# The up product of two MLPs with its operands swapped: weight blocks stationary, both parts of the input moving together

## The reference, cut to what matters

```python
def sq_relu_mlp(x, w_up, w_down):
    h = jax.nn.relu(x @ w_up)
    return (h * h) @ w_down

    # in second_block, for layers 0 and 1
    h = h + rms_norm(sq_relu_mlp(rms_norm(h, mpre), w_up, w_down), mpost)
```

## Time and profile before

| | |
|---|---|
| device time, median of 3 runs | 1142.04 us (1142.02 to 1142.12) |
| device time of the profiled execution | 1141.86 us |
| its span (first to last instruction) | 1140.0 us |
| PE busy | 1130.2 us (99%) |
| PEld busy | 935.3 us (82%) |
| DVE, ACT, POOL busy | 656.9, 622.5, 180.9 us |
| DMA | 204.57 MB, mean 179 GB/s |

### The profile page before, as it was taken

How to read it: one execution, slowest core, us unless ns; L and a number is a source line. 1 busy time by engine, 2 the same in 40 slices (tenths; PEclk the granted TensorE clock), 3 DMA queues, 4 the chain that set the end, 5 groups by cost and what they waited for, 6 DMA issues and landing times.

```text
span 1140.0 us, 14044 instructions
## 1 busy us (share of the span) xinstructions
PE 1130.2 (99%) x5299; PEld 935.3 (82%) x5299; DVE 656.9 (58%) x680; ACT 622.5 (55%) x786; POOL 180.9 (16%) x123
## 2 busy tenths in 40 slices
PE   8999999999999999999999999999999999999998
PEld 7788888888888888888778888888888888888886
DVE  5735668675655544784348565454465776744442
ACT  6655556654867643644478374443355546655331
POOL 1423500000434310000032021110015100211000
PEclk9999999999999999999999999999999999999999
DMA  9644344554554554655335456445545324655530
GB/s 354 237 154 164 131 166 156 194 185 185 185 190 179 192 190 171 231 221 194 139 120 194 150 212 223 176 180 189 198 186 206 128 110 166 221 184 182 184 114 37
DMA packets 30322, 204.57 MB, mean 179 GB/s; under 512 B 3584, under 2 KB 3744, under 8 KB 6592
## 3 DMA queue, kind: packets, MB, share of 16 engines
q1 hardware_dynamic: 28752, 198.75, 48.3%
q0 software_dynamic: 1520, 5.12, 1.4%
HBM read 202.81 MB, written 1.05 MB: 179 GB/s over the span
## 4 chain that ended last, share of the span: by engine, by line
PE 94%; POOL 1%; issue 1%; DVE 1%; ACT 1%; DMA 1%; SPq 0%; DVEq 0%; POOLq 0%; ACTq 0%
PE ps L654 84%; PE aux L726 3%; PE aux L1163 1%; PE ps L776 1%; PE aux L939 1%; PE aux L925 1%; DMA mrows<-in_mem 1%; POOL sc L498 0%; PE aux L1093 0%; PE aux L1044 0%; DVE Wl L1794 0%; ACT Wh L1267 0%; POOL sq L514 0%; DVE sc L1866 0%; ACT prob L1444 0%
## 5 line engine op out<-in xcount | busy, mean ns | idle before, releaser
L1794 DVE TENSOR_TENSOR Wl<-raw,Wh 128x2048 fp32r<-128x2048 f32 x184 | 427.6, 2330 | 326.6 <-ACT Wh L1267 326.3
L654 PE MATMUL ps<-Wh,xT 128*128 128x512 f32 x1920 | 608.2, 393 | 0.0
L1267 ACT ACTIVATE Wh<-raw 128x2048 fp32r<-128x2048 f32 x184 | 349.9, 1907 | 266.5 <-PE ps L654 265.6
L654 PEld LDWEIGHTS ps<-Wh,xT 128*128 128x128 f32 x1920 | 360.5, 188 | 75.1 <-issue 1.2
L654 PE MATMUL ps<-Wl,xT 128*128 128x512 f32 x960 | 373.7, 389 | 0.0
L654 PEld LDWEIGHTS ps<-Wl,xT 128*128 128x128 f32 x960 | 180.4, 188 | 36.4 <-issue 0.5
L654 PE MATMUL ps<-Wh,hTh 128*128 128x512 f32 x256 | 100.1, 391 | 0.0
L654 PE MATMUL ps<-Wh,hTl 128*128 128x512 f32 x256 | 99.7, 389 | 0.0
L654 PE MATMUL ps<-Wl,hTh 128*128 128x512 f32 x256 | 99.6, 389 | 0.0
L654 PEld LDWEIGHTS ps<-Wh,hTl 128*128 128x128 f32 x256 | 48.0, 188 | 10.0
L654 PEld LDWEIGHTS ps<-Wl,hTh 128*128 128x128 f32 x256 | 48.1, 188 | 9.9
(11 more groups left out here) (347 smaller groups left out, 1219.2 us busy)
## 6 DMA issues: line engine op xcount, KB each, us to landing
raw<-in_wstream SPq DMA_DIRECT2D x185, 1024.0 KB, 4.7
grow<-in_post_gains POOLq DMA_DIRECT2D x4, 512.0 KB, 5.5
grow<-in_b_gate POOLq DMA_DIRECT2D x6, 256.0 KB, 3.5
mrows<-in_mem SPq DMA_DIRECT2D x2, 512.0 KB, 5.1
raw<-in_wstream SPq DMA_DIRECT2D x2, 512.0 KB, 6.4
x<-in_x SPq DMA_DIRECT2D x1, 1024.0 KB, 13.3
out<-x SPq DMA_DIRECT2D x4, 256.0 KB, 2.0
rdm<-in_ret_decays POOLq DMA_DIRECT2D x1, 768.0 KB, 6.9
```

The lines of the kernel that those rows point to most:

```text
L654: mm = nc.tensor.matmul(ps[2 * pair + t][:, :], a[:, kt, t * P:(t + 1) * P], w[:, slot, j, :], start=(first and j == 0 and q == 0), stop=( ...
L1267: nc.scalar.activation(Wh[:, slot, 0:nk, :], raw[:, slot, 0:nk, :], ACT.Copy).then_inc(hi_ready, 1)
L1794: nc.vector.tensor_tensor(Wl[:, slot, 0:nk, :], raw[:, slot, 0:nk, :], Wh[:, slot, 0:nk, :].bitcast(F32), ALU.subtract).then_inc(lo_ready, 1)
```

## The change

Up units 0 and 1 stay as they were. For units 2 to 7 of both MLPs:

- **PE.** The 128 x 128 blocks of `Wh` and `Wl` are stationary. For each of four groups of 128 output columns (c = 0 to 3) and each of eight feature steps there is one matmul of `Wh` with both parts of x side by side (512 wide), and one of `Wl` with the high part (256 wide, into the first half of the bank). Column c fills one bank, `column_bank`, whose halves have to be added. The result has output columns on partitions, so it is already transposed: `turned` remains for units 0 and 1 alone. A granule is given back in the last column.
- **`xT`** is laid out with the two parts of each feature step side by side.
- **DVE** adds the halves of each bank into `hrow` (`add_parts`), and subtracts the rounded square from the square for the low part (`rows_low`), both from SBUF, 1024 wide, for the unit before.
- **ACT** applies relu in place in SBUF (`relu`), and later squares the scaled rows in place and rounds them to `hTh` (`rows_high`).
- **POOL** multiplies the rows with `rstd` of each token (`scaled`) instead of squaring. As tokens lie along the row now, `rstd` is needed in every partition: DVE writes two diagonal matrices (`diagonal`), PE multiplies them with ones (`spread_rstd`), DVE copies the result into `spread`, once an MLP.
- Unit 2 and unit 3 are written out, the loop has two turns.

```diff
-        xT = at("xT", [P, 2, DK, TOK], 104, F32R)
-        xTh, xTl = xT[:, 0, :, :], xT[:, 1, :, :]
+        xT = at("xT", [P, DK, 2, TOK], 104, F32R)
+        xTh, xTl = xT[:, :, 0, :], xT[:, :, 1, :]
...
+        def column_bank(m, c):
+            return ps[(2 * U[f"up{m}_0"] + c) % 4]
...
+                def scaled(n, count):
+                    pool.wait_ge(drained["act"], count * 2 + (DRAIN[f"up{m}_0"][1] + 2))
+                    h = hrow[:, n, :, :].rearrange("p b (c t) -> p (b c) t", t=TOK)
+                    nc.gpsimd.tensor_tensor(h, h, spread.unsqueeze(1).broadcast_to([P, 4, TOK]), ALU.mult)\
+                        .then_inc(sem("h_scaled"), 1)
...
                 def up(n, i):
                     name = f"up{m}_{n}"
-                    for q in range(2):
-                        g = G[name] + q
-                        granule(g % RING, i * 4 + (g + 1), xTh, xTl, range(4 * q, 4 * q + 4), U[name] % 2, q == 0, q == 1,
-                                read_out)
+                    for c in range(4):
+                        if isinstance(i, int) and n == 0:
+                            pe.wait_ge(drained["act"], reads(f"up{m}_{c // 2}", c % 2))
+                        else:
+                            pe.wait_ge(sem("column_read"), i * 8 + (4 * n + c + 24 * m - 11))
+                        o = column_bank(m, c)
+                        for kt in range(DK):
+                            g = G[name] + kt // 4
+                            if c == 0 and kt % 4 == 0:
+                                pe.wait_ge(lo_ready, i * 4 + (g + 1))
+                            w = slice(c * P, (c + 1) * P)
+                            nc.tensor.matmul(o[:, :], Wh[:, g % RING, kt % 4, w], xT[:, kt, :, :], start=(kt == 0), stop=False,
+                                             skip_group_check=True)
+                            mm = nc.tensor.matmul(o[:, 0:TOK], Wl[:, g % RING, kt % 4, w], xTh[:, kt, :], start=False,
+                                                  stop=(kt == DK - 1), skip_group_check=True)
+                            if c == 3 and kt % 4 == 3:
+                                mm.then_inc(gran_used, 1)
+                            elif kt == DK - 1:
+                                mm.then_inc(half_done if c == 1 else sem("column_done"), 1)
...
+                def spread_rstd():
+                    pe.wait_ge(sem("rstd_diag"), 2 * m + 2)
+                    o = open_aux(f"rs{m}")
+                    for t in range(2):
+                        mm = nc.tensor.matmul(o[:, t * P:(t + 1) * P], K("ones"), spread[:, t * P:(t + 1) * P], start=True, stop=True)
+                    done(mm, f"rs{m}")

                 turned(0)
-                with pe.Fori(1, 4) as i:
+                spread_rstd()
+                up(0, 1)
+                turned(1)
+                up(1, 1)
+                with pe.Fori(2, 4) as i:
                     up(0, i)
-                    turned(-1, i)
                     up(1, i)
-                    turned(0, i)
...
+                def rows_high(n, i):
+                    act.wait_ge(sem("h_scaled"), i * 2 + (n + 6 * m - 1))
+                    h = hrow[:, n % 2, :, :].rearrange("p b c -> p (b c)")
+                    nc.scalar.activation(h, h, ACT.Square).then_inc(sem(f"h{m}_rows"), 1)
+                    act.wait_ge(sem(f"h{m}_rows"), i * 2 + (n + 1))
+                    dst = hTh[:, :, :].rearrange("p (n k) t -> p n (k t)", k=4)
+                    nc.scalar.activation(dst[:, i * 2 + n, :], h, ACT.Copy).then_inc(sem(f"h{m}T_hi"), 1)
...
+                def columns(n, i, between):
+                    name = f"up{m}_{n}"
+                    relu(n, i, 0)
+                    between()
+                    split(G[name] + RING, i)
+                    relu(n, i, 1)
+                    split(GEND[name] - 1 + RING, i)
...
+                columns(0, 1, lambda: h_high(1))
+                columns(1, 1, lambda: rows_high(0, 1))
+                with act.Fori(2, 4) as i:
+                    columns(0, i, lambda: rows_high(-1, i))
+                    columns(1, i, lambda: rows_high(0, i))
                 split(G[f"down{m}_0"] + RING)
-                h_high(7)
+                rows_high(1, 3)
...
+                    o = column_bank(m, c)
+                    nc.vector.tensor_reduce(hrow[:, n, c // 2, (c % 2) * TOK:(c % 2 + 1) * TOK],
+                                            o[:, :].rearrange("p (q t) -> p t q", q=2), AX.X, ALU.add).then_inc(sem("column_read"), 1)

+                def columns(n, i, between):
+                    for c in range(3):
+                        add_parts(n, i, c)
+                    between()
+                    add_parts(n, i, 3)
+                    up(n, i)
```

More of the change, by code:

```diff
@@ L177, in plan_aux @@
     use("x3T", [0, 1, 2, 3])
-    for n in range(8):
-        use(f"h0T{n}", [2 * n % 4, 2 * n % 4 + 1])
+    use("h0T0", [0, 1])
+    use("rs0", [2])
+    use("h0T1", [2, 3])
     use("x4T", [0, 1, 2, 3])
@@ L191, in plan_aux @@
     use("x5T", [0, 1, 2, 3])
-    for n in range(8):
-        use(f"h1T{n}", [2 * n % 4, 2 * n % 4 + 1])
+    use("h1T0", [0, 1])
+    use("rs1", [2])
+    use("h1T1", [2, 3])
     return plan
@@ L369, in build @@
         hrow = at("hrow", [P, 2, 2, C], R + 64)
+        spread0 = CONST["chunk_upto"][0]
+        spread = cst[:, spread0:spread0 + TOK]
         junk = at("junk", [P, D], R + 72)
@@ L604, in squares, with one @@
             def squares(m):
-                def one(n, count):
-                    pool.wait_ge(drained["act"], 2 * count + (DRAIN[f"up{m}_0"][1] + 2))
-                    h = hrow[:, n % 2, :, :]
+                def one(n):
+                    pool.wait_ge(drained["act"], 2 * n + (DRAIN[f"up{m}_0"][1] + 2))
+                    h = hrow[:, n, :, :]
                     nc.gpsimd.tensor_tensor(h, h, h, ALU.mult).then_inc(sem(f"h{m}_rows"), 1)
-                one(0, 0)
-                one(1, 1)
-                with pool.Fori(1, 4) as i:
+                def scaled(n, count):
[3 more added lines that the diff above has]
+                        .then_inc(sem("h_scaled"), 1)
+                one(0)
+                one(1)
+                wait_read(pool, f"rs{m}")
+                scaled(0, 2)
+                scaled(1, 3)
+                with pool.Fori(2, 4) as i:
                     for n in range(2):
-                        one(n, i * 2 + n)
+                        scaled(n, i * 2 + n)
             after_mix("p2", "x3", (1, reads("reto1", 1)))
@@ L679, in kts_of, with product @@
                 return range(k0, k0 + KTS[g])
-            def product(name, operand, before=None, leave=0):
+            def product(name, operand, before=None, leave=0, bank_free=None):
                 th, tl = operand
@@ new lines, in turned @@
+                def turned(n):
+                    pe.wait_ge(sem(f"h{m}_rows"), n + 1)
+                    for b in range(2):
+                        turn(f"h{m}T{n}", b, [(kk * TOK + t * P, hrow[:, n, t, (2 * b + kk) * P:(2 * b + kk + 1) * P])
+                                              for kk in range(2) for t in range(2)])
+                def spread_rstd():
[4 more added lines that the diff above has]
+                    done(mm, f"rs{m}")
@@ L1175, in go_on @@
                     def go_on():
-                        if q == 1:
-                            turned(7)
-                        wait_operand(f"h{m}T{q}", range(2))
-                    return go_on
-                product(f"down{m}_0", (hTh, hTl), before={q: before(q) for q in range(8)})
-                product(f"down{m}_1", (hTh, hTl), leave=RING)
+                        if q < 2:
+                            wait_operand(f"h{m}T{q}", range(2))
+                        else:
+                            pe.wait_ge(sem("h_low"), 6 * m + q - 1)
@@ L1183, in mlp @@
+                    return go_on
+                product(f"down{m}_0", (hTh, hTl), before={q: before(q) for q in range(8)}, bank_free=column_free(0))
+                product(f"down{m}_1", (hTh, hTl), leave=RING, bank_free=column_free(1))
                 tile_by_tile(steps_of([f"down{m}_1"], (hTh, hTl)),
@@ L1680, in up, with relu @@
                         nc.scalar.activation(hrow[:, n % 2, t, :], bank(name, t), ACT.Relu,
                                              scale=S(f"{xname}_rstd", t, t + 1)).then_inc(drained["act"], 1)
-                    split(GEND[name] - 1 + RING, i)
-                def h_high(n, i=None):
+                    split(GEND[name] - 1 + RING)
+                def relu(n, i, b):
+                    act.wait_ge(sem("column_read"), i * 8 + (4 * n + 2 * b + 2 + 24 * m - 8))
+                    h = hrow[:, n, b, :]
+                    nc.scalar.activation(h, h, ACT.Relu).then_inc(drained["act"], 1)
@@ L1685, in h_high @@
+                def h_high(n):
                     dst = hTh[:, :, :].rearrange("p (n b k) t -> p n b k t", b=2, k=2)
                     for b in range(2):
```

(18 more changed lines are left out.)

59 lines of the change are left out of this document (27 added, 32 removed).

## The result

| | median | ratio to before |
|---|---|---|
| before | 1142.09 us | |
| changed kernel | 1144.55 us | 1.0021 [1.0013, 1.0028] |

What follows compares the result with a forecast made beforehand. PE's stream was taken to bound the kernel, then a DVE-ACT-POOL round of 11.95 us against PE's 11.20. Saving 1.65 us in each MLP took 1141.86 to 1138.6, forecast as 1138.8 us; range 1134.8 to 1147.5.

Steps and rivals of the forecast that it cites:

- a closed round of DVE, ACT and POOL: Per changed unit, in-order queues tie these engines into a round of 11.95 us, where PE needs 11.20.
- PE's own sum: PE alone, per MLP: dearer matmul pairs (0.350 us each) and `spread_rstd` against six transpose groups dropped: -3.0 us, both -6.1.
- rival 3: On PE, loads aren't hidden behind 256-wide matmuls: 0.415 us a pair, 13.3 a unit, +18.9, total 1161 us; chance 0.06.
- rival 1: DVE-ACT-POOL round of 10.6 us keeps up with PE, no waits: -6.1, or -7.2 at 0.347 a pair; chance 0.16.
- Adds of halves, roundings, relu, square, copy, low part: DVE and ACT operations: `add_parts` 0.683 us, roundings 1.92 or 1.81, relu 0.63, square and copy 1.06 each, `rows_low` 1.22.
- rival 2: DVE's `add_parts` is dear: gain nothing at 0.83 us, total +10.3 at 1.22; 1144 to 1152 us; chance 0.22.
- The port: POOL and DVE exclude each other when DVE has two SBUF inputs; after the wait POOL takes 1.75 us, DVE 2.14.
- Hand-overs of 0.03: Between ACT and DVE in the round, one engine's end to the next one's start takes 0.03 us.
- Rival 4: Nothing measurable: hand-overs of 0.1, or square and copy 0.3 us longer, make the round about 12.3: -1.5 to +1; chance 0.21.
- Sum: Whole program: 1.65 us saved in each MLP, -3.3 from 1141.86 gives 1138.6; median 0.18 above, so 1138.8 us.
- The delay at the start: First changed units: ACT's `h_high(1)` waits for `turned(1)`, ending about 695.7; add 3 of the second unit ends 709.5.

Runs made afterwards that it cites:

- the fourth experiment: Changed kernel with one more wait, so POOL starts `scaled` only after DVE's second subtraction of weights of the unit; all work kept: 1134.59 us, 0.9935 of the kernel before.
- The first experiment: Changed kernel with POOL multiplying the rows by themselves, one SBUF tensor instead of two, scaling by rstd left out: 1139.62 us, 0.9978 of the kernel before.

## Why the prediction was wrong

The direction was wrong; the mechanism, a closed round of DVE, ACT and POOL that sets PE's pace, was the forecast one. The steps that failed are two terms of its sum: POOL's `scaled`, taken for 1.75 us behind its wait and measured at 2.27, and, far smaller, the hand-overs, taken for 0.03 us and measured at 0.13 to 0.15 in two places.

- *PE's own sum: right.* 0.350 was taken for a pair, 0.347 measured; the loads are hidden (rival 3 is out). With the waits gone the program gains 7.5 us; the price of rival 1 at 0.347 a pair was 7.2. The 0.11 us that a unit is shorter than forecast (11.09 against 11.20) bring nothing while the round sets the pace.
- *Adds of halves, roundings, relu, square, copy, low part: right.* `add_parts` took 0.678 us against 0.683, so rival 2 is out; the bound of 1.22 was never near.
- *The port: right as a mechanism, wrong in size.* "1.75 for the one" was taken from POOL squaring `hrow`, a product of one tensor with itself. `scaled` reads two tensors. The row that is nearest to it stood in the trace of before and was not used; POOL by line and shape (busy us, mean ns of one, idle before), of the kernel before:

```profile
L547 POOL TENSOR_TENSOR GG<-go,GG 128x1024 f32<-128x1024 f32 x1 | 2.4, 2398 | 0.0
```

  Two different tensors of 1024 take 2.40 us, and POOL takes exactly that in the fourth experiment, where it starts later. The sentence that failed is the one that calls `scaled` "a 1024-wide product like the square that it replaces: 1.90 alone". 0.5 us were missing in a round that was already 0.85 us over PE's 11.1 and is run through five times an MLP. The first experiment prices it at 4.93 us.
- *Hand-overs of 0.03: wrong in two places.* The row used was that of a subtraction with a fixed address, and such hand-overs take 0.03 in the loop too; the two whose operation has an address that depends on the loop's counter take 0.13 to 0.15. The written-out loop prices them at 0.74 us. Rival 4 named such a lengthening of the hand-overs, at a round of 12.3; both errors together made 12.6, beyond it.
- *Sum.* 1138.8 + 4.93 + 0.74 = 1144.47, against 1144.55 measured. That the two add up is argued, as each was measured alone. The trace says it another way: `down` was forecast to start at 752.3 and starts at 754.97, 2.7 us late, and the last adds of the units before it ended 0.2, 1.0, 1.6 and 2.3 us late (709.70, 722.39, 734.99, 747.61). Twice 2.7 us is 5.3 or so of the 5.75 us by which the forecast missed; where the last 0.4 us arise isn't shown.
- *The delay at the start: right.* The add 3 of the second changed unit was forecast to end at 709.5 and ended at 709.70. The range held the time only because it had to reach to the rival with dear adds; that rival is not why, so this is luck.

## What to carry to other kernels

When a change ties several engines into a closed round with a slack of a few per cent, each duration in it counts as often as the round turns, so each needs the row with the same number of tensors and the same source, not only the same width: 0.5 us was worth 4.9 here and nothing outside the round. For operations of POOL and DVE that exclude each other, ask at which moment each is released; here it paid to start POOL when DVE turned to adds that read PSUM, and that one wait was worth 10 us. And before a factor of each token is carried through a layout in which it is awkward, look whether a norm behind it cancels it.

## What the runs showed of the hardware that was not expected

- POOL's product of 1024 fp32 elements takes 1.90 us with one tensor and 2.40 with two, also if the second is a block repeated by its pattern (2.41 in the kernel before with ones). A second input of one value for each 128 elements costs nothing on top (1905 ns), so it isn't the number of inputs alone:

```profile
L507 POOL TENSOR_TENSOR GG<-GG,sc 128x1024 f32<-128x1024 f32 x1 | 1.9, 1905 | 0.1
```

- Where POOL has to wait for DVE, it needs less after the wait than when it starts freely: 1.76 and 2.27 us against 1.90 and 2.40 for 1024 elements, 1.16 against 1.30 for 512 (L569 of the kernel before), 0.13 to 0.14 less.
- An operation in the hardware loop whose address depends on the counter started 0.10 to 0.12 us later after a wait on ACT and DVE than the same operation written out; one with a fixed address did not (0.03).
- PE had waited 5.0 us an MLP where the idle times in its timeline add up to 3.8: the sum of gaps understates a wait, the distance between the units' starts doesn't.
